# Neighbourhood attention on one core: transpositions first, values of the step in front, bias and scores of the step two ahead

## The reference, cut to what matters

```python
# q, k, v: (1, 512, 8, 64); kc, vc: 256 context tokens; kh = 8 rows, so that all 8 rows are seen by every query
def row_block(r):
    ...
    s_loc = einsum('bnqhd,binkhd->bhnqik', qr, kr) * scale + bias      # relative position bias
    s_loc = where(mask, s_loc, -inf)                                   # 16 columns around the query
    s_ctx = einsum('bnqhd,bjhd->bhnqj', qr, kc) * scale
    p = softmax(concatenate([s_loc, s_ctx], -1))
    return einsum('bhnqik,binkhd->bnqhd', p_loc, vr) + einsum('bhnqj,bjhd->bnqhd', p_ctx, vc)
y_c = o_c * silu(cz)
# layer 0 also: softmax_attn(q_ctx, k_ctx, v_ctx) * silu(cz_ctx) for the 256 context tokens
```

## Time and profile before

| | us |
|---|---|
| median of 3 executions | 3300.82 |
| the profiled execution | 3300.97 |
| its span, first to last instruction | 3299.3 |
| TensorE matmuls busy | 3112.5 (94%) |
| VectorE busy | 1516.3 (46%) |
| ScalarE busy | 1193.5 (36%) |
| mean granted TensorE clock, share of full | 0.981 |

### The profile page before, as it was taken

One profiled execution on the slowest core, in us unless ns is written; L12 is line 12 of the kernel. 1 busy time (PEld: TensorE's weight loads), 2 busy tenths in 40 slices (PEclk: granted clock), 3 DMA queues, 4 the chain that ended last, 5 costly groups with the idle time before them and its releaser, 6 DMA issues.

```text
span 3299.3 us, 39408 instructions
## 1 busy us (share of the span) xinstructions
PE 3112.5 (94%) x15890; PEld 2498.0 (76%) x15890; DVE 1516.3 (46%) x2084; ACT 1193.5 (36%) x1926; POOL 70.6 (2%) x118
## 2 busy tenths in 40 slices
PE   7999999999999989989999799979999899989888
PEld 5778888777788878768886588758877788668666
DVE  4655445544645562662425432253346543542344
ACT  4344323434534451362324321252233533431342
POOL 1000000000000000000000000100000000000100
PEclk9999999999999999999999799999999999999999
DMA  4233232331322211001110011311120112021222
GB/s 168 102 141 111 106 115 102 122 119 34 133 102 89 99 61 64 33 23 64 52 59 13 20 64 52 99 38 64 40 83 33 54 58 90 7 83 64 96 68 77
DMA packets 41259, 247.26 MB, mean 75 GB/s; under 512 B 5480, under 2 KB 5488, under 8 KB 17312
## 3 DMA queue, kind: packets, MB, share of 16 engines
q1 hardware_dynamic: 30528, 204.30, 17.6%
q0 software_dynamic: 10592, 40.99, 3.7%
HBM read 241.07 MB, written 4.19 MB: 74 GB/s over the span
## 4 chain that ended last, share of the span: by engine, by line
PE 86%; DVE 6%; ACT 4%; issue 2%; DMA 1%; SPq 0%; DVEq 0%; ACTq 0%; POOLq 0%
PE PS L726 14%; PE PS L727 14%; PE PS L728 14%; PE PS L707 7%; PE PS L706 6%; PE PS L708 6%; PE PS L672 2%; PE PS L674 2%; PE PS L673 2%; PE PS L1109 1%; DVE SMALL L2183 1%; PE PS L1136 1%; PE PS L907 1%; PE PS L1017 1%; DMA W<-in_w 1%
## 5 line engine op out<-in xcount | busy, mean ns | idle before, releaser
L726 PE MATMUL PS<-HHX,WHX 128*128 128x512 f32 (+1 forms) x1600 | 564.7, 353 | 35.0 <-DVE WLM L2033 31.0
L727 PE MATMUL PS<-HL,WHX 128*128 128x512 f32 (+1 forms) x1600 | 565.3, 353 | 0.0
L1403 ACT ACTIVATE WHX<-W 128x2048 fp32r<-128x2048 f32 x108 | 186.1, 1723 | 611.5 <-DMA W<-in_w 389.8
L726 PEld LDWEIGHTS PS<-HHX,WHX 128*128 128x128 f32 x1600 | 307.0, 192 | 79.7 <-issue 32.9
L728 PE MATMUL PS<-HHX,WLX 128*128 128x512 f32 (+1 forms) x1024 | 354.2, 346 | 0.0
L727 PEld LDWEIGHTS PS<-HL,WHX 128*128 128x128 f32 x1600 | 305.5, 191 | 41.0
L2033 DVE TENSOR_TENSOR WLX<-W,WHX 128x2048 fp32r<-128x2048 f32 x60 | 137.5, 2292 | 374.1 <-ACT WHX L1403 374.1
L707 PE MATMUL PS<-HL,WH 128*128 128x512 f32 x672 | 265.4, 395 | 0.0
L706 PE MATMUL PS<-HH,WH 128*128 128x512 f32 x672 | 263.3, 392 | 0.0
L708 PE MATMUL PS<-HH,WL 128*128 128x512 f32 x672 | 261.7, 389 | 0.0
L2033 DVE TENSOR_TENSOR WL<-W,WH 128x2048 fp32r<-128x2048 f32 x68 | 155.9, 2292 | 221.8 <-ACT WH L1403 221.8
(11 more groups left out here) (451 smaller groups left out, 5904.7 us busy)
## 6 DMA issues: line engine op xcount, KB each, us to landing
W<-in_w SPq DMA_DIRECT2D x172, 1024.0 KB, 4.7
XC<-in_wm POOLq DMA_DIRECT2D x12, 1024.0 KB, 5.1
H<-in_wm POOLq DMA_DIRECT2D x12, 1024.0 KB, 5.7
W<-in_wb SPq DMA_DIRECT2D x24, 512.0 KB, 3.2
W<-in_w SPq DMA_DIRECT2D x8, 768.0 KB, 4.0
PR<-in_nbias POOLq DMA_DIRECT2D x12, 256.0 KB, 2.9
ARENA<-in_nbias POOLq DMA_DIRECT2D x12, 256.0 KB, 2.9
X<-in_x SPq DMA_DIRECT2D x2, 1024.0 KB, 6.2
```

The source lines that it names most:

```text
L726: pe.matmul(dst, wh[:, s, c], hi[:, k, t0:t1], start=k == 0, stop=False)
L727: pe.matmul(dst, wh[:, s, c], lo[:, k, t0:t1], start=False, stop=False)
L1403: act.activation(dst[:, s, 0:n], W[:, s, 0:n], ACT.Copy).then_inc(wh_ready[s], 1)
```

## The change

TensorE's loop issues `transposes(e)` first, then the `values` of step e-1, then `scores(e+2)`; the `values` of the last step stand behind the loop. VectorE's `post` moves from the loop of step e+1 to that of step e+2, and the last two stand behind the loop. ScalarE's order, VectorE's order of `probs` and `maxima`, all semaphores and all buffers stay as they are.

```diff
         scores(steps[0])
         scores(steps[1])
         for e in steps:
+            transposes(e)
+            if e["s"]:
+                values(steps[e["s"] - 1])
             if e["s"] + 2 < len(steps):
                 scores(steps[e["s"] + 2])
-            transposes(e)
-            values(e)
+        values(steps[-1])
...
         maxima(steps[0])
         maxima(steps[1])
-        late = None
         for e in steps:
             probs(e)
             if e["s"] + 2 < len(steps):
                 maxima(steps[e["s"] + 2])
-            if late:
-                post(late)
-            late = e if e["last"] else None
-        post(late)
+            if e["s"] >= 2 and steps[e["s"] - 2]["last"]:
+                post(steps[e["s"] - 2])
+        for e in steps[-2:]:
+            if e["last"]:
+                post(e)
```

## The result

The changed kernel takes 3370.22 us (median of 4, 3369.37 to 3376.58) against 3300.54 us of the kernel before (4 runs): ratio 1.0212, 95% interval 1.0196 to 1.0228, 69.7 us slower. The forecast was 3374 us with a range of 3344 to 3409. The profiled execution is the slowest of the four: 3376.58 us, span 3374.9 us.

What follows compares the result with a forecast made beforehand. The prediction took TensorE, with 86% of the chain of waits, to bound the kernel. To 3301 us it added 50 us of net stalls and 23 us of low clock spells: 3374 us, range 3344 to 3409.

Steps and rivals of the forecast that it cites:

- What goes: TensorE's `values` stop waiting 0.86 us for ScalarE's copies in 34 of 36 steps; 31.0 us removed, the rest counted separately.
- the tail's term: Last step of each stage: the last values wait 1.28 us for values and copies in a row.
- What is late next: Transpositions of e+1 wait for VectorE's probs(e+1), behind maxima(e+2), which wait for scores just issued: 2.11 us a step.
- The last term: From the start of VectorE's multiplication to TensorE's first transposition: 0.67 us.
- The step: One step in the two changed stages takes 6.34 us in place of 5.09: 4.23 of TensorE work plus 2.11 stall.
- the chain: From scores through VectorE's maxima, reciprocal and multiplication to the next transpositions, no longer covered by TensorE work: 2.11 us.
- The sum below the clock: All stalls gained and lost in both stages, before any fall of the clock: 50 us slower (44.7 + 4.6 + 0.5).
- `post`: Moved on VectorE ahead of probs(e+1), it adds 0.60 us six times and 0.33 us three times: 4.6 us.
- The clock: TensorE's clock falls to half behind four in nine of the new gaps: 14 spells of 1.6 us, 23 us.
- the clock holds: Rival: the same stalls in both stages but no low clock spells, 3351 us; chance 0.20.
- The clock falls in every step: Rival: 32 spells of 1.6 us in the two stages, 3402 us; chance 0.18 for this or worse.
- The stall goes and none comes: Rival: TensorE's waits for the copies go and no new stall appears, 3280 us; chance 0.03 for faster.

Runs made afterwards that it cites:

- experiment 1: The changed kernel with VectorE issuing probs(e+1) ahead of maxima(e+2): 3285.58 us against 3299.97 us for the kernel before, ratio 0.9959.
- the filler of 8: The changed kernel with 8 transpositions of the identity, useless work, on TensorE behind the scores of each step: 3343.48 us.
- experiment 3: The changed kernel with the post of step e-2 ahead of maxima(e+2) instead of behind it: 3368.32 us, ratio to the kernel before 1.0209.
- the filler of 4: The changed kernel with 4 transpositions of the identity, useless work, on TensorE behind the scores of each step: 3353.1 us.

## Why the prediction was right, point by point

- **What goes.** Right: L1017 waits for the copies only in the last step of each stage, 1.24 us in layer 0, as the tail's term of 1.28 had it.
- **What is late next.** Right in mechanism and shown by experiment 1: without `maxima` ahead of `probs` the stall isn't there. The size: 3.05 us from the scores' start to the transpositions' start against 3.17 forecast (1.17 + 1.14 + 0.19 + 0.67), so a stall of 1.99 in place of 2.11. The last term was the wrong one: 0.54 us (2165.10 to 2165.64) in place of 0.67, taken from a step in which the transpositions were the first of the stage. 32 times 0.12 is 3.8 us too much.
- **The step.** Forecast 6.34 us, measured 6.16 where the clock is full. Besides the chain, the four groups were put too high: 4.23 us, where experiment 1's steps without a gap take 4.16. The transpositions start 1.94 us ahead of the `values` in the earlier trace rows and cost 1.02, so the stall that went was 0.92 us by starts, not 0.86: 36 times 0.06 is some 2 us more gained than forecast.
- **The sum below the clock.** Forecast 50 us. From the trace: 70.4 us of new idle time, and in the tails 0.79 and 1.24 us for each stage, 4.1, less 36 times 0.84, 30.2, is 44.3. The forecast less the two errors above (3.8 and 2) gives the same, and so do the 43.5 us that are left with the filler of 8, which still has one low spell.
- **`post`.** 0.60 and 0.33 us on the chain, as forecast, by the intervals in the trace. Context steps' own transpositions start 0.14 us later, three times, 0.4 us for the 0.5 forecast.
- **The clock.** Forecast 14 spells of 1.6 us, 23 us. Behind 17 of the 34 gaps in the loops the clock fell, and twice more, one fall at the end of each stage. The filler's answer is 26.7 us, or 1.7 for each fall spared, where the forecast had 1.6. One in two, where the rows elsewhere gave four in nine. That this share carried over from nine gaps in other code was luck: no rule stood behind it, and the gap's length, which the prediction held against "the clock holds" ("nine of them over 2.4 us"), didn't make falls more frequent. The clock's part, put too low, and the chain's, put too high, cancel in part in the sum: 3374 against 3370.22.
- **The rivals.** "The clock holds" is out (0.88, 0.87); the kernel with 8 fillers is about what it would have been, 3343.5 us where the rival had 3351. "The clock falls in every step" is out: 17 of 34. "The stall goes and none comes" came true only with a second edit, experiment 1.

The clock also reached beyond the stages. In layer 1, in code that the change doesn't touch, the clock now fell at two gaps where it hadn't, and the fall at 2815.82 of the kernel before (2810 to 2820) is missing. One of the two: the gap of 2.47 us ahead of L907 had kept full clock before; in the changed kernel the stretch behind the same gap (2566.66 to 2569.13) reads

```profile
2570.00:2574.00 4.00, 4.00 (x18) 2.79 (x16) 3.62 (x5) 2.91 (x7) 0.00 (x0) 0.57 0.00 0
```

That may be part of why four executions of one kernel spread over 7 us, and five of experiment 3 over 11. Only one execution of each has a trace, so it isn't shown, but the mean granted clock goes with the time: 0.970 in the execution of 3376.58 us and 0.972 or 0.973 in the other three, 0.973 in that of 3362.83 us and 0.970 in that of 3374.2.

## What to carry to other kernels

When one engine's order of work is changed, write down the order of each engine it trades with, and look for an instruction that now waits for what has just been issued while the next thing needed stands behind it. Here TensorE's new order lost 70 us with VectorE's old order and gained 14 with one swap there (22 with two more edits): ready work should stand ahead of an engine's wait for the newest work. A regular idle gap of some 2 us can cost more than its length, since the clock may fall behind it; a filler kernel tells the two parts apart.

## What was not expected of the hardware

- The same gap in the same code (2.47 us ahead of L907) led to a fall of the clock in one kernel and not in the other. Within the loops of this stage 17 of 34 gaps of 1.9 to 2.5 us were followed by a fall, 16 of them gaps of 1.92 or 1.93 us and only one a gap of over 2 us; with the filler of 4, four of eight of 1.92 to 1.94 us, and none of the 28 of 0.8 to 1.7 us.
- Float32 transpositions of the identity held the full clock (1.00 in layer 0 with 16 more of them in each step).
- Added work on the busiest engine made the kernel faster: 1.0 us a step, 26.7 us in all.
